# Expert products of a grouped MoE in four chunks of 32 rows instead of two of 64, with the expert loads counted in order

## The reference

```python
scores = sigmoid(t @ router_w)                        # t: 640 x 1024, 16 experts in 4 groups
best = argmax(group scores)                           # one group per token
idx = top_k(where(in_group, scores + router_b, -inf), 2)
gates = sum(one_hot(idx) * wts[..., None], axis=1)    # wts: their scores over their sum
a, b = einsum('td,edf->tef', t, w_gate), einsum('td,edf->tef', t, w_up)   # 1024 -> 256 for every expert
act = silu(a) * b * gates[:, :, None]
moe = einsum('tef,efd->td', act, w_down)              # 256 -> 1024
x = x + gate2 * moe
```

## Time and profile before

| | |
|---|---|
| time, median of 3 runs | 1115.02 us (1114.5 to 1117.04) |
| the profiled execution: span from first to last instruction | 1112.5 us |
| instructions | 17990 |
| TensorE's granted clock, mean | 0.998 (2.4 GHz) |
| busy: TensorE matmul, weight load | 95%, 53% |
| busy: VectorE, ScalarE, GpSimd | 51%, 35%, 18% |
| moved by DMA | 241.47 MB, mean 217 GB/s |
| gate and up matmuls (L1120) | 1856 records, 412.8 us of them |
| down matmuls (L1160) | 464 records, 106.0 us in the first group |

### The profile page before, as it was taken

How to read it: one execution, slowest core, us unless ns; L and a number is a source line. 1 busy time by engine, 2 the same in 40 slices (tenths; PEclk the granted TensorE clock), 3 DMA queues, 4 the chain that set the end, 5 groups by cost and what they waited for, 6 DMA issues and landing times.

```text
span 1112.5 us, 17990 instructions
## 1 busy us (share of the span) xinstructions
PE 1058.8 (95%) x5918; PEld 589.1 (53%) x5919; DVE 572.7 (51%) x1223; ACT 389.0 (35%) x800; POOL 204.8 (18%) x313
## 2 busy tenths in 40 slices
PE   3999999999999899999999999899999979999996
PEld 0566564555544455555546655555644445555552
DVE  0334545665345754454574545476724674534557
ACT  0332224444211244444333222454511134444540
POOL 0133456000000100100152435800000011001003
PEclk9999999999999999999999999999999999999999
DMA  9940006668801799999981000557540379999917
GB/s 351 361 138 1 1 9 238 217 222 302 331 19 40 248 378 377 381 358 366 332 289 41 1 1 0 187 194 279 207 149 38 112 260 376 381 379 380 376 78 284
DMA packets 129064, 241.47 MB, mean 217 GB/s; under 512 B 12304, under 2 KB 92192, under 8 KB 122864
## 3 DMA queue, kind: packets, MB, share of 16 engines
q1 hardware_dynamic: 115904, 194.83, 50.1%
q0 software_dynamic: 7056, 25.69, 6.3%
q10 hardware_dynamic: 6048, 20.22, 4.5%
HBM read 213.63 MB, written 27.10 MB: 216 GB/s over the span
## 4 chain that ended last, share of the span: by engine, by line
PE 80%; DMA 8%; DVE 3%; issue 3%; SPq 3%; POOL 1%; ACT 1%; DVEq 0%; POOLq 0%; ACTq 0%
PE bank L1120 17%; PE pair L1045 12%; PE pair L1160 9%; PE pair L762 7%; PE pair L777 6%; DMA big<-ada_w 4%; PE pair L895 4%; PE pair L794 3%; PE bank L811 3%; PE bank L931 3%; PE bank L672 3%; PE pair L1090 3%; PE bank L910 2%; PE bank L746 2%; DMA big<-y_rows,big 2%
## 5 line engine op out<-in xcount | busy, mean ns | idle before, releaser
L1120 PE MATMUL bank<-big,actT 128*64 (+1 forms) x928 | 206.3, 380 | 2.4 <-ACT actT L1445 1.9
L1120 PE MATMUL bank<-actT 128*64 128x256 f32 x928 | 206.5, 381 | 0.0
L1120 PEld LDWEIGHTS bank<-big,actT 128*64 128x64 f32 x928 | 124.7, 137 | 83.1 <-issue 26.0
L1045 PE MATMUL pair<-big,actT 128*128 128x512 f32 x320 | 142.7, 598 | 0.0
L1120 PEld LDWEIGHTS bank<-actT 128*64 128x64 f32 x928 | 124.7, 137 | 0.0
L1160 PE MATMUL pair<-big 128*64 (+1 forms) x464 | 106.0, 598 | 0.7 <-ACT big L1470 0.7
L1045 PEld LDWEIGHTS pair<-big,actT 128*128 128x128 f32 x320 | 59.0, 190 | 67.8 <-issue 67.6
L762 PE MATMUL pair<-big,actT 128*128 128x384 f32 (+1 forms) x320 | 93.6, 447 | 0.3 <-ACT actT L1218 0.2
L1988 DVE TENSOR_REDUCE mx<-pair 128x1 f32<-128x640 f32 x64 | 52.7, 823 | 72.0 <-PE pair L896 71.9
L1642 POOL DMA_INDIRECT big<-h_rows,big x29 | 27.7, 956 | 304.3 <-PE pair L1090 286.9
L762 PEld LDWEIGHTS pair<-big,actT 128*128 128x128 f32 x320 | 59.5, 190 | 29.3 <-ACT actT L1218 1.9
(11 more groups left out here) (274 smaller groups left out, 1628.9 us busy)
## 6 DMA issues: line engine op xcount, KB each, us to landing
big<-ada_w SPq DMA_DIRECT2D x48, 1024.0 KB, 5.0
big<-w_gate SPq DMA_DIRECT2D x32, 1024.0 KB, 13.1
big<-w_up SPq DMA_DIRECT2D x32, 1024.0 KB, 16.3
big<-w_down SPq DMA_DIRECT2D x32, 1024.0 KB, 14.5
y_rows<-big ACTq DMA_DIRECT2D x28, 512.0 KB
big<-w_out SPq DMA_DIRECT2D x4, 2048.0 KB, 13.4
big<-mod_rows SPq DMA_DIRECT2D x16, 512.0 KB, 9.2
h_rows<-big ACTq DMA_DIRECT2D x10, 512.0 KB, 2.7
```

Source lines behind the costliest of these rows:

```text
L1045: m = mm(dst, actT[:, k, t * P:(t + 1) * P], vw.wo[n][:, k, :], start=(k == order[0]), stop=(k == order[-1]))
L1120: m = mm(dst[CH * h:CH * h + CH, 0:DE], xgT[:, k, CH * h:CH * h + CH], weights(h, k * 2 * DE + lo, DE), start=(k == 0), stop=(k == DC - 1) ...
```

## The change

A step keeps its 128 rows, but they are now four chunks of `CH` = 32, and a set of matmuls is four side by side, of 32 array columns each. `QUEUE` names where each takes its weights from: chunk 0 from the ring at a register's address, chunks 1 and 2 (of one expert; the slots are laid so) from ScalarE's copy, chunk 3 from VectorE's copy. So each of the two engines now copies all weights of one expert per step, in six pieces of 128x1024 (L1501 and L2299), into three buffers each: a piece may be written when TensorE has used the one three before, which the new semaphore `used` counts, once per piece. Experts get at least as many chunks that this pairing holds (`least`), and the first step is all of expert 0: one matmul over the whole array width per block, no copies (`products(0, ..., True)`). The tables `eland` and `eslot` tell per step and source the landing to wait for and the place. The loads are counted by part in expert order on three semaphores (`ld_wg`, `ld_wu`, `ld_wd`), and each waits until the same part of the expert before has landed. w_gate and w_up are laid out in the ring with the contraction index split as `(p k)` instead of `(k p)`, so that a partition reads 8 KB in one run; the rows of the second norm are written in the matching order (`by_row`). The places in the ring are (1, 2, 3, 0, 4) for (1, 2, 3, 4, 0). Expert 3 is loaded behind the second norm's last rows, ahead of the wait for `r_gate`. Step 0 is written out ahead of the loop on ScalarE and VectorE too, and TensorE lists the steps' rows (`list_rows`) behind the turning of the first rows. Line numbers in this section and its diff's code are those of the changed kernel.

```diff
-CH = 64
-NSTEP = 18
+CH = 32
+NSTEP = 19
+TILES = [(c_ * CH, CH) for c_ in range(P // CH)]
+QUEUE = [0, 1, 1, 2]
+FIRST_CHUNKS = P // CH
...
+NCHUNK = FIRST_CHUNKS * NSTEP
+NQ = 3
 NSLOT = NSTEP * P
 RING = 5
+PLACES = (1, 2, 3, 0, 4)
+PIECE = D
+NPIECES = 6
+USED_0 = 4
...
+    least[:, 0] = -1
+    least[1::2, 1] = -1
+    least[0, 0:FIRST_CHUNKS] = -1
...
-        half_gu = flat[:, 0:4096]
-        half_d = at(30720, 2 * D)
+        parts = [None,
+                 [flat[:, 0:PIECE], flat[:, 2 * PIECE:3 * PIECE], flat[:, 3 * PIECE:4 * PIECE]],
+                 [flat[:, PIECE:2 * PIECE], at(30720, PIECE), at(30720 + PIECE, PIECE)]]
...
         def slot_of(e):
-            return (e + 1) % RING
-        def loads_of(s, e):
-            return fifths(e + (RING + 1 - s if s > 0 else 1)) * 48
-        def loads_before(s, l):
-            return 48 + l * 48 * sum(slot_of(e) == s for e in range(NE))
+            return PLACES[e % RING]
+        def used_at(n, i):
+            return n * NPIECES + (i + 1 + USED_0)
+        def used_in(steps, i):
+            return steps * NPIECES + (i + 1 + USED_0 - NPIECES)
+        def landed(l, e):
+            return 16 * (NE * l + e + 1)
...
+        def by_row(a, lo=0, hi=P):
+            return a.rearrange("q (k p) -> q p k", k=DC)[:, lo:hi, :]
...
                     if e >= RING:
                         steps = sp.value_load(fin[0:1, e - RING:e - RING + 1], min_val=1, max_val=NSTEP)
-                        sp.wait_ge(gu_mm, steps * 2)
-                    sp.dma_start(wgu[s][:, :, 0:DE], w_gate[l, e].rearrange("(k p) n -> p k n", p=P)).then_inc(ld_w[s], 16)
-                    sp.dma_start(wgu[s][:, :, DE:2 * DE], w_up[l, e].rearrange("(k p) n -> p k n", p=P)).then_inc(ld_w[s], 16)
+                        sp.wait_ge(used, used_in(steps, 1))
+                    if e > 0:
+                        sp.wait_ge(ld_wg, landed(l, e - 1))
+                    sp.dma_start(wg[s], w_gate[l, e].rearrange("(p k) n -> p (k n)", k=DC)).then_inc(ld_wg, 16)
                     if e >= RING:
-                        sp.wait_ge(dn_mm, steps)
-                    sp.dma_start(wd[s][:, :, :], w_down[l, e].rearrange("(k p) n -> p k n", p=P)).then_inc(ld_w[s], 16)
...
                 sp.wait_ge(op_x, L(op_x) + 2 * NT)
+                sp.wait_ge(h_ready, L(h_ready) + 2 * NT)
+                load_expert(3)
                 sp.wait_ge(r_gate, L(r_gate) + 1)
                 sp.wait_ge(r_slot, L(r_slot) + 1)
-                load_expert(3)
                 load_expert(4)
...
                 stay_awake(a7, 4)
-                for j in range(2 * NT):
-                    if j % NT == 0:
-                        pe.wait_ge(r_one, L(r_one) + j // NT + 2)
-                    m = mm(pair[1][:, 0:NSTEP], onep[:, j, :], oneb[:, j, :], start=(j == 0), stop=(j == 2 * NT - 1))
-                m.then_inc(r_pe1, 1)
-                stay_awake(a7, 2)
+                stay_awake(a7, 3)
+                def list_rows():
+                    for j in range(2 * NT):
+                        if j % NT == 0:
+                            pe.wait_ge(r_one, L(r_one) + j // NT + 2)
+                        m = mm(pair[1][:, 0:NSTEP], onep[:, j, :], oneb[:, j, :], start=(j == 0), stop=(j == 2 * NT - 1))
+                    m.then_inc(r_pe1, 1)
...
+                def weights_of(n, i, land, place, first):
+                    if i % 2 == 0:
+                        pe.wait_ge((ld_wg, ld_wu, ld_wd)[i // 2], land)
+                    if not first:
+                        for w in w_s:
+                            pe.wait_ge(w, n * NPIECES + i)
+                    def weights(c, lo, cols):
+                        if QUEUE[c] == 0:
+                            return wring[:, place, i * PIECE + lo:i * PIECE + lo + cols].rearrange("p a n -> p (a n)")
+                        return parts[QUEUE[c]][i % 3][:, lo:lo + cols]
+                    return weights
+                def products(n, land, place, first):
+                    tiles = [(0, P)] if first else TILES
                     pe.wait_ge(b_ta, n + 1)
                     pe.wait_ge(b_td, n + 1)
-                    pe.wait_ge(w_a, n * 3 + 1)
-                    pe.wait_ge(w_d, n * 3 + 1)
-                    gate_up(tb4, 0).then_inc(gu_mm, 1)
-                    pe.wait_ge(w_a, n * 3 + 2)
-                    pe.wait_ge(w_d, n * 3 + 2)
-                    gate_up(tb5, DE).then_inc(gu_mm, 1)
-                    return weights
-                def rest(n, last, weights):
-                    w_a, w_d = w_s
+                    for i in range(4):
+                        weights = weights_of(n, i, land, place, first)
+                        dst = (tb4, tb5)[i // 2]
+                        for k in range(4 * (i % 2), 4 * (i % 2) + 4):
+                            for c, (lo, m_) in enumerate(tiles):
+                                m = mm(dst[lo:lo + m_, 0:DE], xgT[:, k, lo:lo + m_], weights(c, k % 4 * DE, DE),
+                                       start=(k == 0), stop=(k == DC - 1), tile_position=(0, lo), skip_group_check=True)
+                        m.then_inc(used, 1)
...
+                    for k in range(2):
+                        weights = weights_of(n, 4 + k, land, place, first)
+                        pe.wait_ge(b_atc, n * 2 + (k + 1))
+                        for j in range(2):
+                            for c, (lo, m_) in enumerate(tiles):
+                                m = mm(pair[1][lo:lo + m_, j * HALF:(j + 1) * HALF], acT[:, k, lo:lo + m_],
+                                       weights(c, j * HALF, HALF), start=(k == 0), stop=(k == 1), tile_position=(0, lo),
+                                       skip_group_check=True)
+                        m.then_inc(used, 1)
...
+                list_rows()
+                land_0, place_0 = landed(l, 0), slice(slot_of(0), slot_of(0) + 1)
+                products(0, land_0, place_0, True)
...
+                def part_place(n):
+                    land = act.value_load(eland[0:1, bass.ds(n + NSTEP, 1)], min_val=16, max_val=landed(DEPTH - 1, NE - 1))
+                    place = act.value_load(eslot[0:1, bass.ds(n + NSTEP, 1)], min_val=0, max_val=RING - 1)
+                    return land, wring[:, bass.ds(place, 1), :].rearrange("p a n -> p (a n)")
+                def part_copy_w(n, part, i):
+                    land, slot = part
+                    if i % 2 == 0:
+                        act.wait_ge((ld_wg, ld_wu, ld_wd)[i // 2], land)
+                    act.wait_ge(used, used_at(n, i - 3))
+                    f(parts[1][i % 3], slot[:, i * PIECE:(i + 1) * PIECE], ACT.Copy).then_inc(w_a, 1)
+                def step(n, first, last):
+                    if not first:
+                        part = part_place(n)
+                        part_copy_w(n, part, 3)
+                    act.wait_ge(used, used_at(n, 1))
...
+                    rows_copy(n + 2)
+                    if first:
+                        act.wait_ge(r_fin, L(r_fin) + 1)
+                        act.wait_ge(r_slot, L(r_slot) + 1)
+                    part = part_place(n + 1)
+                    for i in range(3):
+                        part_copy_w(n + 1, part, i)
...
+                    h2 = by_row(xn[t % 2])
+                    link(v.scalar_tensor_tensor(h2, plain(x[:, t, :]), rs[:, NT + t:NT + t + 1], plain(vw.G[:, c2, :]),
+                                                ALU.mult, ALU.mult))
+                    v.tensor_tensor(h2, h2, plain(vw.S[:, c2, :]), ALU.add).then_inc(h_ready, 1)
...
+                ts(single[:, 1:NE + 1], nb, 1.0, None, ALU.is_equal)
+                link(ts(start_m, startx, 0.0, None, ALU.add))
+                stt(slot1, by_expert(startx[:, 0:NE]), float(CH), pos, ALU.mult, ALU.add)
+                link(ts(start_m, start_m, FIRST_CHUNKS - 1, None, ALU.bitwise_and))
+                ts(at_one, start_m[:, 0:NE], 1.0, None, ALU.is_equal)
...
+                    if not first:
+                        part = part_place(n)
+                        for i in range(3, NPIECES):
+                            part_copy_w(n, part, i)
...
+                        part = part_place(n + 1)
+                        part_copy_w(n + 1, part, 0)
...
+                        part_copy_w(n + 1, part, 1)
+                    ve.wait_ge(used, used_at(n, 5))
...
                     tt(yb, pair[1][:, :], yb, ALU.mult).then_inc(b_yd, 1)
-                with ve.Fori(0, n_more) as i:
-                    step(i, False)
-                step(n_more, True)
+                    part_copy_w(n + 1, part, 2)
```

284 lines of the change are left out of this document (140 added, 144 removed).

## The result

The changed kernel takes 1098.16 us (median of 4 runs, 1095.22 to 1099.6) beside 1115.98 us of the kernel before: a ratio of 0.9836, 95% interval 0.9818 to 0.9854. That is 17.8 us off, where 36 were forecast: half of the gain is missing, and the time lies just above the range, whose upper end was 1098. The profiled execution's span is 1095.8 us, 16.7 less than before.

What follows compares the result with a forecast made beforehand. Bound by TensorE, with DMA loads close behind in the expert stage. -48.5 + 5 + 0.5 + 2.8 + 4.4 = -35.8 us; 1112.5 - 35.8 + 2.5 = 1079 us, range 1069 to 1098.

Steps and rivals of the forecast that it cites:

- Part 1: Expert stage: 12 and 13 steps for 14 and 15, each staying 12.12 us long, -48.5 us.
- rival (c): TensorE's sets of four: weight loads of column tiles not hidden, 4.2 us per step, +98 us, 1177 us; chance 0.06.
- (d): Rival on the step count: minima and padding eat the chunks, 29 steps with dearer hand-offs, 1125 us; chance 0.02.
- Part 2: Copies and hand-offs of ScalarE and VectorE to TensorE in each step: 0.2 us x 23 = +5 us.
- All fit, by 0.1 to 0.5 us: Claim that every copy and hand-off in a step meets TensorE's clock; piece 3 copied to 5.1, wanted 5.2.
- The bound of 0.8 us a step: Upper bound for the hand-offs' cost per step, if the tight ones are each missed a little.
- Part 3: Expert weight loads: runs of 8 KB for 1 KB give 9.8 us per expert, cover holds; +0.5 us taken.
- Part 4: Work ahead of each layer's first step: later blend difference and gather, +1.6 and +1.2 us, ends 0 and 3 each.
- The blend difference comes some 5 us later: VectorE ahead of the first step: from 391.8 to near 397, with the first activation product behind it.
- Part 5: Last step of each layer: early tables ahead of VectorE's copies make TensorE wait, +2.3 and +2.1 us.
- VectorE's tail has 1.0 us of waiting for the last gather that takes some of it: Second layer's end: that waiting absorbs part of the last step's delay, +3.4 becoming +2.1 us.
- Rival (a): Hand-offs missed: a step 0.8 us longer instead of 0.2, +14 us, 1093; with strided h2 writes 1098; chance 0.22.

## Why the prediction was wrong

- **Part 1, fewer steps: right.** 12 and 13 steps, 48.4 us. On TensorE a set of four costs what a set of two did, so rival (c) is out, and so is (d). The rule of the Trainium skill, *TensorE: Matmul & The Clock Gate* (section *Part 3: Packing small matmuls*), that weight loads overlap products in flight only where the row group differs, would have made it so; this trace disagrees, at 0.21 us a set with one row group.
- **Part 2, the hand-offs: the chain was right, the sum mis-sized.** "All fit, by 0.1 to 0.5 us" failed at the one with 0.1: piece 3 started at 4.3 and ended at 5.4, for 5.1, in a good step, and in 5 of 23 steps a register read took up to 1.1 us longer. The term was 0.2 us x 23 = 5; it is 10.9, of which 1.2 is the wait at L1178, and against the loops without those waits 14.4. The bound of 0.8 us a step held. The experiment shows the cause: with piece 3 behind the store the waits and the 14 us go.
- **Part 3, loads: right.** 400 to 428 GB/s in windows of 12 and 3 us (418 at 424, 400 at 500), no wait of TensorE for a load, and with 1 KB runs waits that made four steps 9 us longer and the loops 4.4. The rule of the Trainium skill, *DMA: Bandwidth & Descriptors* (section *Where 436 GB/s comes from*), some 358 GB/s from HBM, disagrees with this trace too.
- **Part 4, ahead of the first step: the step that failed most.** I took 2.8 us for both layers, at most 6; it was 12.6, of which 1.0 us lies ahead of this stage. "The blend difference comes some 5 us later" was 7.9. Of these, 5.4 are there when the comparison starts: the 1.0 us from ahead, 0.7 of the permuted write (1.99 us for 1.29), which was costed at 0, 2.6 of small operations, as worked out, and the first rows' copy, which now stands ahead of the listing's tables. Behind it the comparison and sum took 2.8 us, no more than I had worked out, but the operations from there to r_slot 4.0 us for 1.3: 17 more of them, where I had counted "a few of the 15"; two copies that stood in between (L2191, L2240 before) are gone from there, which took some of it back. The gather, whose later landing I mentioned and didn't price, landed 3.5 us later. And the idle time of 4.2 and 4.0 us let the clock fall, 1.7 and 1.4 us more in the down products. With the gates moved away 4 us of it went, with a few products in the waits 2.8.
- **Part 5, the last step: the wait right, its consequences left out.** +1.9 for 2.3 in the first layer; in the second the wait is the 3.4 us that was forecast, and 1.2 us more are the clock over the fourth piece, +4.6 in all (two of the variants had the same wait and no fall of the clock, and a last step of 15.1 us for 16.5). The tail didn't take 1.3 back but cost 1.7 by the clock. "VectorE's tail has 1.0 us of waiting for the last gather that takes some of it" failed because that gather was held up by the same fourth piece.
- Rival (a) had the mechanism of the loops, but it was told as the loops' alone, at +14 us, and 1098 with strided writes; that the time came out at 1098 too is luck. The real excess of 19 us is 6 in the loops (0.5 for the loads, not needed, goes off), 10 in the first steps and 4 in the last steps with the tail. The range should have added mishaps that can come true together.
